# Attention probabilities transposed as products with the identity on two column strips, in one core's decoder kernel

## The chip, the core and the metric

The kernel runs on one core of a Trainium2 chip. The metric is the device time of one execution in microseconds, the median of several runs. TensorE (PE in the profile, with its weight loads as PEld) does the products and transposes, VectorE (DVE) and ScalarE (ACT) the elementwise work, GpSimd (POOL) and SyncE (SP) mostly issue transfers.

## The reference

Two decoder layers over 512 tokens of width 1024. Each is half a SwiGLU block, a mixing block with sparse attention (8 heads of 64), a pooling branch and attention into 256 memory tokens (4 heads of 64), and another half SwiGLU block. What the change touches is the last product of both attentions:

```python
logits = jnp.einsum('bqhd,bqkhd->bhqk', qb, kg).astype(jnp.float32) * (HEAD_DIM ** -0.5)
logits = jnp.where(valid[:, None], logits, -jnp.inf)
p = jax.nn.softmax(logits, axis=-1).astype(vg.dtype)
return jnp.einsum('bhqk,bqkhd->bqhd', p, vg)
...
p = jax.nn.softmax(logits, axis=-1).astype(mv.dtype)
out = jnp.einsum('bhsm,bmhd->bshd', p, mv)
```

## The kernel before

Activations lie transposed: features on the partitions, tokens along the columns. The large products (the SwiGLU blocks and the projections) split both operands into a high and a low part of type fp32r and add three products; their weights stream from memory through a ring of four slots. They take up most of the time.

The attention of a layer is cut into 48 units. A unit `n` is one head of one tile of 128 queries; the tiles go from the last to the first, and each has 8 sparse heads and then 4 memory heads. A sparse head of query tile `i` has `i + 1` blocks of 128 keys, a memory head has two. So a layer has 8 x (4 + 3 + 2 + 1) + 16 x 2 = 112 blocks, and the two layers 224.

Each unit passes four stages:

- `logits(n)` on TensorE, two units side by side: the product over 64 rows, for the two heads of a pair in the two halves of the rows (`64*128` in the profile's shapes: 64 rows by 128 columns of the array).
- `mask_and_max(n)` on VectorE (L1364) adds the mask and takes the maximum; `exps(n)` on ScalarE (L1086) takes the exponential and writes `prob[n % 4]` (in t1 or in buffers of their own, so the profile names it `t` or `prob`).
- `transpose_p(n)` on TensorE (L821): each block of probabilities, queries by keys, is transposed to keys by queries into `bank[2 + n % 2]`. `copy_pt` then copies the bank to `pt[n % 4]`, for even units on ScalarE (L1079), for odd ones on VectorE (L344).
- `times_v(n)` on TensorE: for each block and each head of the pair the values (128 keys by 64) stand in the array, the transposed probabilities are streamed, and the two heads' results go to partitions 0 to 63 and 64 to 127 (`128*64`).

After a group of heads, `spread_sums(g)` spreads the inverse row sums in the same layout: a product of a broadcast column of `rinv` (128 by 64) with the identity, even units to the lower half of `bank[7]` and odd units to the upper half. There are 8 groups in a layer. ScalarE copies the result to `rt` (L1095), VectorE multiplies it in (L1382), and both split the result (L1102, L1392).

TensorE's order is written out by hand. One step of the loop takes two units, and so the stages of different units follow each other:

```python
for n in range(0, UNITS + LAG + 2, 2):
    ...
    if n < UNITS:
        logits(n)
    if n - 2 in group_after:
        spread_sums(group_after[n - 2])
    if 0 <= n - LAG < UNITS:
        transpose_p(n - LAG)
        transpose_p(n - LAG + 1)
    if 0 <= n - LAG - 2 < UNITS:
        times_v(n - LAG - 2)
```

`LAG` is 4 and `UNITS` 48. Transposes are followed directly by `times_v` in the steps n = 6 to 50, 23 times in a layer, and they directly follow `spread_sums` 8 times in a layer (n = 10, 14, 22, 26, 34, 38, 46, 50). Two pooling products (`pool_map`, with `wpool`) stand ahead of the logits of the steps 28 and 32; they share `bank[7]` and `bank[6]` with the sums and values, so they wait for the copy to `rt`. While the softmax runs, ScalarE also rounds weights for the output projection (`round_ahead`, L931 and L932, after the units 9, 11, 21 and 23).

`mm(out, lhsT, rhs)` is the plain product on TensorE (L472 is its line for all callers). All operands of the transposes, of `spread_sums` and of `times_v` are of type fp32.

Of the kernel before, what the change touches and what calls it, by code (L numbers as in the profile page):

```python
# [21 lines left out]
P = 128  # L22
# [3 lines left out]
HD = 64  # L26
# [43 lines left out]
C_ID = 0  # L70
# [35 lines left out]
def build(nc, x_t, mem_t, weights, pool_w, params, consts, out):  # L106
# [85 lines left out]
    prob = [t1[:, 0:T], t1[:, T:2 * T]] + \  # L192
# [7 lines left out]
    bank = [nc.alloc_psum_tensor(f"bank{i}", [P, 512], f32) for i in range(8)]  # L200
# [5 lines left out]
    def con(at, n=1, parts=P):  # L206
        return const[0:parts, at:at + n]
# [96 lines left out]
    def unit(n):  # L304
        s, h = divmod(n, UNITS_PER_TILE)
        i = TT - 1 - s
        is_mem = h >= HEADS
        return i, (h - HEADS if is_mem else h), is_mem, (MT if is_mem else i + 1)
# [44 lines left out]
    with nc.Block() as block:  # L353
# [111 lines left out]
        def _(pe):  # L465
# [5 lines left out]
            def mm(out_, lhsT, rhs, start=True, stop=True):  # L471
                return nc.tensor.matmul(out_, lhsT, rhs, start=start, stop=stop, skip_group_check=True)  # L472
# [126 lines left out]
            def mix(l):  # L599
# [73 lines left out]
                for i in range(TT):  # L673
                    last = mm(bank[3][:, TT + 4 * i:TT + 4 * i + 4], iw[0:4, i * P:(i + 1) * P],
                              con(C_ID, 4, 4))
# [9 lines left out]
                for i in range(MT):  # L685
                    last = mm(bank[2][:, i:i + 1], sq[:, i * P:(i + 1) * P], con(C_ONES, 1))
# [44 lines left out]
                for part, hr in enumerate((hr_hi, hr_lo)):  # L731
                    for s in range(QT):
                        rows = slice(s * STRIP, (s + 1) * STRIP)
                        last = mm(bank[4 + s][:, :], spread[rows, :], hr[rows, :], part == 0, part == 1)
# [7 lines left out]
                for c in range(MQT):  # L742
                    for i in range(MT):
                        last = nc.tensor.transpose(bank[4][:, c * MEM + i * P:c * MEM + (i + 1) * P],  # L744
                                                   mk_n[:, i * MEM + c * P:i * MEM + (c + 1) * P],
                                                   con(C_ID, P))
# [68 lines left out]
                def transpose_p(n):  # L815
                    i, h, is_mem, blocks = unit(n)
                    pe.wait_ge(p_ready, l * UNITS + (n + 1))
                    if n >= 2:
                        pe.wait_ge(pt_ready[n % 2], l * (UNITS // 2) + n // 2)
                    for b in range(blocks):  # L820
                        last = nc.tensor.transpose(bank[2 + n % 2][:, b * P:(b + 1) * P],  # L821
                                                   prob[n % 4][:, b * P:(b + 1) * P], con(C_ID, P))
                    last.then_inc(ptp_done, 1)

                def times_v(n):
# [37 lines left out]
                for n in range(0, UNITS + LAG + 2, 2):  # L863
                    if n in POOL_UNITS:
                        pool_map(POOL_UNITS.index(n))
# [9 lines that stand above are left out]
                    for b in FILL.get(n, ()):  # L875
                        fill(b)
# [641 lines left out]
```

## Time and profile before

| | us |
|---|---|
| median of 3 runs | 1970.55 (1969.13 to 1972.46) |
| the profiled execution, its own time | 1967.57 |
| its span | 1965.5 |
| TensorE busy | 1918.9 (98%) |
| ScalarE busy | 1082.7 (55%) |
| VectorE busy | 614.1 (31%) |

The span goes from the first instruction to the last; the rest of the execution's own time, 2.1 us, lies around it. Busy time of TensorE is read from modelled ends: one product's time runs into the next one's, so in a dense stretch the distance between the starts of two runs of products says what one costs, and not the time of one. The attention units of the first layer lie from 528 to 584 us of the span, those of the second from 1500 to 1556 us.

### The profile page before, as it was taken

The page shows a single profiled execution, that of the slowest core. Times are in us where ns is not written, and L with a number is a line of the kernel's source. Part 1 is how long each engine was busy: PE and PEld are TensorE (multiplying, and loading weights), DVE is VectorE, ACT ScalarE, POOL GpSimd, SP SyncE. Part 2 cuts the span into 40 slices and gives each one's busy share as a digit, 9 for nine tenths or more (in the row PEclk, how much of TensorE's full clock was granted, in tenths as well). Part 3 has the DMA queues.
Part 4 walks back from the last instruction along what each step waited for, and adds up shares of the span by engine and source line. Part 5 has one row for each costly group of instructions (what it writes and reads, how often), then busy time and mean ns, then how long its engine had stood idle before and what let it go on. Part 6 is the DMA issues. An engine that isn't in the chain of part 4 may idle for free.

```text
span 1965.5 us, 27449 instructions
## 1 busy us (share of the span) xinstructions
PE 1918.9 (98%) x9148; PEld 1559.4 (79%) x9148; DVE 614.1 (31%) x1176; ACT 1082.7 (55%) x1391; POOL 347.6 (18%) x400
## 2 busy tenths in 40 slices
PE   6999999999899999999999999999998999999999
PEld 4888888887668888888878888888876688888887
DVE  3222210367662322220052222004677542222101
ACT  6655543565475755553375556336656566565432
POOL 1111111112511111111111111111125011111110
PEclk9999999999999999999999999999999999999999
DMA  8988888788236888888868888888781279888887
GB/s 219 215 190 191 194 193 193 184 197 193 76 87 150 199 197 191 192 193 192 194 162 201 191 193 189 199 192 199 177 205 48 70 173 221 192 193 193 194 190 184
DMA packets 97703, 354.07 MB, mean 180 GB/s; under 512 B 10976, under 2 KB 11232, under 8 KB 97376
## 3 DMA queue, kind: packets, MB, share of 16 engines
q0 software_dynamic: 47232, 171.99, 49.2%
q1 hardware_dynamic: 49824, 178.81, 27.7%
q10 hardware_dynamic: 576, 2.36, 0.3%
q8 instruction: 40, 0.66, 0.1%
q14 instruction: 31, 0.25, 0.0%
HBM read 179.05 MB, written 2.10 MB: 92 GB/s over the span
## 4 chain that ended last, share of the span: by engine, by line
PE 94%; DMA 2%; DVE 1%; issue 1%; ACT 1%; DVEq 0%; SPq 0%; ACTq 0%; POOLq 0%
PE bank L472 92%; PE bank L821 1%; DMA w_lo<-raw 1%; DMA raw<-weights 1%; ACT w_lo L932 0%; DMA x<-x_t 0%; DVE z L1315 0%; DVE mk_n L1321 0%; ACT prob L1086 0%; DVE t L1364 0%; ACT kv L1049 0%; ACT t L1086 0%; ACT w_hi L931 0%; DVE pt L344 0%; PE bank L744 0%
## 5 line engine op out<-in xcount | busy, mean ns | idle before, releaser
L931 ACT ACTIVATE w_hi<-raw 128x1024 fp32r<-128x1024 f32 x329 | 348.4, 1059 | 617.6 <-PE bank L472 592.1
L472 PE MATMUL bank<-h_hi,w_hi 128*128 128x512 f32 x1664 | 656.0, 394 | 15.6 <-ACT h_hi L903 13.6
L472 PE MATMUL bank<-h_hi,w_lo 128*128 128x512 f32 x1664 | 651.5, 392 | 5.7 <-DMA w_lo<-raw 5.7
L472 PE MATMUL bank<-h_lo,w_hi 128*128 128x512 f32 x1664 | 634.3, 390 | 0.0
L395 POOL DMA_DIRECT2D w_lo<-raw x328 | 282.6, 863 | 1556.5 <-ACT w_lo L932 1517.3
L472 PEld LDWEIGHTS bank<-h_hi,w_hi 128*128 128x128 f32 x1664 | 314.9, 189 | 88.5 <-ACT h_hi L903 15.1
L472 PEld LDWEIGHTS bank<-h_hi,w_lo 128*128 128x128 f32 x1664 | 314.7, 189 | 71.9 <-DMA w_lo<-raw 6.2
L472 PEld LDWEIGHTS bank<-h_lo,w_hi 128*128 128x128 f32 x1664 | 313.2, 188 | 66.2 <-issue 1.4
L932 ACT ACTIVATE w_lo<-raw 128x1024 fp32r<-128x1024 f32 x329 | 342.8, 1042 | 0.0
L472 PE MATMUL bank<-a_hi,w_hi 128*128 (+1 forms) x832 | 324.6, 390 | 0.0
L472 PE MATMUL bank<-a_lo,w_hi 128*128 (+1 forms) x832 | 323.8, 389 | 0.0
L472 PE MATMUL bank<-a_hi,w_lo 128*128 (+1 forms) x832 | 323.7, 389 | 0.0
L1168 DVE SCALAR_TENSOR_TENSOR x<-bank,x 128x512 f32<-128x512 f32 x48 | 32.7, 691 | 512.9 <-PE bank L472 512.9
L472 PEld LDWEIGHTS bank<-a_hi,w_hi 128*128 128x128 f32 x832 | 156.2, 188 | 33.7 <-issue 1.4
L472 PEld LDWEIGHTS bank<-a_hi,w_lo 128*128 128x128 f32 x832 | 156.2, 188 | 32.5
L472 PEld LDWEIGHTS bank<-a_lo,w_hi 128*128 128x128 f32 x832 | 156.2, 188 | 32.0
L1186 DVE TENSOR_TENSOR t<-bank,r 128x512 f32<-128x512 f32 x88 | 60.8, 690 | 382.1 <-PE bank L472 382.1
L931 ACT ACT_TABLE_LOAD x45 | 57.7, 1283 | 126.8 <-PE bank L472 119.1
L1183 DVE TENSOR_TENSOR t<-bank,r 128x512 f32<-128x512 f32 x88 | 60.8, 691 | 161.2 <-PE bank L472 160.3
L1192 DVE TENSOR_TENSOR a_lo<-t,a_hi 128x512 f32 x88 | 60.9, 692 | 111.2 <-ACT a_hi L950 111.2
L1190 DVE TENSOR_TENSOR t<-t,t 128x512 f32<-128x512 f32 x88 | 60.9, 692 | 11.6 <-ACT t L947 1.6
L947 ACT ACT_TABLE_LOAD x44 | 56.5, 1283 | 0.8
(143 smaller groups left out, 1226.2 us busy)
## 6 DMA issues: line engine op xcount, KB each, us to landing
raw<-weights SPq DMA_DIRECT2D x332, 512.0 KB, 4.7
w_lo<-raw POOLq DMA_DIRECT2D x328, 512.0 KB, 5.8
x<-x_t SPq DMA_DIRECT2D x4, 512.0 KB, 7.1
mem<-mem_t ACTq DMA_DIRECT2D x2, 1024.0 KB, 7.4
out_t<-x SPq DMA_DIRECT2D x8, 256.0 KB, 2.2
const<-consts SPq DMA_DIRECT2D x1, 481.5 KB, 10.0
wpool<-pool_w ACTq DMA_DIRECT2D x2, 128.0 KB, 7.2
par<-params SPq DMA_DIRECT2D x1, 38.0 KB, 1.8
```

The source lines that it names most:

```text
L395: G.dma_start(w_lo[:, s], raw[:, s], accum_op=ALU.add).then_inc(w_ready[pos], 16)
L472: return nc.tensor.matmul(out_, lhsT, rhs, start=start, stop=stop, skip_group_check=True)
L821: last = nc.tensor.transpose(bank[2 + n % 2][:, b * P:(b + 1) * P], prob[n % 4][:, b * P:(b + 1) * P], con(C_ID, P))
L931: nc.scalar.activation(w_hi[:, s], raw[:, s], ACT.Copy).then_inc(w_hi_done, 1)
L932: nc.scalar.activation(w_lo[:, s], raw[:, s], ACT.Copy, scale=-1.0)\
L947: nc.scalar.activation(g, g, ACT.Silu).then_inc(silu_ready, 1)
L1168: V.scalar_tensor_tensor(out=chunk(x, j), in0=bank[j][:, :], scalar=scale, in1=chunk(x, j), op0=ALU.mult, op1=ALU.add)\
L1183: V.tensor_tensor(out=g, in0=bank[2 * half][:, :], in1=r[:, :], op=ALU.mult).then_inc(gate_ready, 1)
L1186: V.tensor_tensor(out=h, in0=bank[2 * half + 1][:, :], in1=r[:, :], op=ALU.mult).then_inc(gu_free, 1)
L1190: V.tensor_tensor(out=h, in0=g, in1=h, op=ALU.mult).then_inc(prod_ready, 1)
L1192: V.tensor_tensor(out=a_lo[:, ds(f * T + half * T, T)], in0=h, in1=a_hi[:, ds(f * T + half * T, T)].bitcast(f32), op=ALU.subtract).then_in ...
```

## The change

A block is no longer transposed with `nc.tensor.transpose` over the whole array, but with two plain products with the identity: the probabilities of 64 keys (128 queries by 64 keys) stand in the array, the identity (128 by 128) is streamed, and the result, 64 keys by 128 queries, goes to partitions 0 to 63 for the first half of the keys and 64 to 127 for the second.

```diff
                     for b in range(blocks):
-                        last = nc.tensor.transpose(bank[2 + n % 2][:, b * P:(b + 1) * P],
-                                                   prob[n % 4][:, b * P:(b + 1) * P], con(C_ID, P))
+                        for half in range(2):
+                            keys = b * P + half * HD
+                            last = mm(bank[2 + n % 2][half * HD:(half + 1) * HD, b * P:(b + 1) * P],
+                                      prob[n % 4][:, keys:keys + HD], con(C_ID, P))
                     last.then_inc(ptp_done, 1)
```

On TensorE, in the fourth of the steps with transposes (n = 10, query tile 3), the instructions stand as follows before (-) and after (+). `prob_95` and `prob_96` are the probabilities of the two units, `rinv` the inverse row sums, `pt_91` and `v` the operands of `times_v`; the numbers behind the names are the shape of the result.

```order
 L472 MATMUL bank<-const,rinv 64x128 x8
 L819 REGISTER_ALU
-L821 MATMUL bank<-const,prob_95 128x128 x4
-L817 REGISTER_ALU
-L821 MATMUL bank<-const,prob_96 128x128 x4
+L472 MATMUL bank<-const,prob_95 64x128 x8
+L817 REGISTER_ALU
+L472 MATMUL bank<-const,prob_96 64x128 x8
 L472 MATMUL bank<-pt_91,v 64x128
 L472 MATMUL bank<-pt_92,v 64x128
```

Nothing has moved; the eight transposes of two units have become 16 products of the shape of those on either side of them.

The same on TensorE in the step after the first group's sums of memory heads, where a unit has two blocks (n = 14).

```order
 L472 MATMUL bank<-const,rinv 64x128 x4
 L819 REGISTER_ALU
-L821 MATMUL bank<-const,prob_95 128x128 x2
-L817 REGISTER_ALU
-L821 MATMUL bank<-const,prob_96 128x128 x2
+L472 MATMUL bank<-const,prob_95 64x128 x4
+L817 REGISTER_ALU
+L472 MATMUL bank<-const,prob_96 64x128 x4
 L472 MATMUL bank<-pt_91,kv 64x128
```

Four transposes have become eight products. No other engine's instructions change.

## Rows read from the trace of the kernel before

**Rows 1.** The page: busy time by engine, and the chain that ended last

```profile
PE 1918.9 (98%) x9148; PEld 1559.4 (79%) x9148; DVE 614.1 (31%) x1176; ACT 1082.7 (55%) x1391; POOL 347.6 (18%) x400
...
PE 94%; DMA 2%; DVE 1%; issue 1%; ACT 1%; DVEq 0%; SPq 0%; ACTq 0%; POOLq 0%
```

**Rows 2.** Busy time in stretches (granted clock behind POOL): units of either layer

```profile
528.00:584.00 56.00, 53.03 (x542) 37.95 (x542) 39.10 (x136) 47.21 (x138) 18.80 (x23) 1.00 0.33 77
...
1500.00:1556.00 56.00, 52.62 (x538) 37.73 (x539) 39.47 (x137) 47.41 (x137) 19.36 (x23) 1.00 0.32 77
```

**Rows 3.** TensorE's groups by shape, whole span (x counts records)

```profile
L472 PE MATMUL bank<-pt,v 128*64 128x128 f32 x320 | 24.5, 283 | 0.0
L821 PE MATMUL bank<-const,t 128*128 128x128 f32 x112 | 18.9, 286 | 2.7 <-DVE pt L344 2.6
L821 PE MATMUL bank<-const,prob 128*128 128x128 f32 x112 | 17.6, 285 | 0.3
L472 PE MATMUL bank<-const,rinv 128*64 128x128 f32 x192 | 14.0, 281 | 0.0
...
L472 PE MATMUL bank<-pt,kv 128*64 128x128 f32 x128 | 10.5, 285 | 0.0
```

**Rows 4.** TensorE in order of time: start, us, line, shape, records (query tile 3)

```profile
533.49 1.09 PE L821 MATMUL bank<-const,t 128*128 128x128 f32 x8
534.51 1.09 PE L472 MATMUL bank<-pt,v 128*64 128x128 f32 x16
535.54 0.38 PE L472 MATMUL bank<-a_hi 64*128 64x256 f32 x2
...
536.09 1.09 PE L472 MATMUL bank<-const,rinv 128*64 128x128 f32 x16
537.11 1.09 PE L821 MATMUL bank<-const,prob 128*128 128x128 f32 x8
```

**Rows 5.** TensorE in order of time, query tile 2

```profile
553.11 0.88 PE L821 MATMUL bank<-const,prob 128*128 128x128 f32 x6
553.92 0.88 PE L472 MATMUL bank<-pt,v 128*64 128x128 f32 x12
554.72 0.50 PE L472 MATMUL bank<-a_hi 64*128 64x256 f32 x4
...
555.27 0.66 PE L821 MATMUL bank<-const,t 128*128 128x128 f32 x4
555.86 0.88 PE L472 MATMUL bank<-pt,v 128*64 128x128 f32 x12
...
558.01 0.66 PE L821 MATMUL bank<-const,prob 128*128 128x128 f32 x4
...
560.62 1.10 PE L472 MATMUL bank<-u,wpool 128*128 128x512 f32 x2 [1.38 <-ACT rt L1095]
```

**Rows 6.** TensorE's waits from 528 to 584 us: total, times, longest

```profile
PE bank L472 <- ACT rt L1095: 1.4, 1, 1.4
PE bank L821 <- DVE pt L344: 1.3, 3, 0.8
```

**Rows 7.** ScalarE in order of time: idle before (in brackets), around TensorE's longest wait

```profile
550.59 0.49 ACT L1079 ACTIVATE pt<-bank 128x384 f32<-128x384 f32 x1 [0.32 <-PE bank L821]
562.75 0.38 ACT L1079 ACTIVATE pt<-bank 128x256 f32<-128x256 f32 x1 [1.54 <-PE bank L821]
```

**Rows 8.** TensorE and VectorE around the second wait

```profile
543.85 1.13 DVE L1392 TENSOR_TENSOR a_lo<-yt,a_hi 128x512 fp32r<-128x512 f32 x1 [0.25 <-ACT a_hi L1102]
...
546.00 0.52 PE L821 MATMUL bank<-const,t 128*128 128x128 f32 x3 [0.76 <-DVE pt L344]
```

**Rows 9.** TensorE's three other waits inside a run of transposes, query tiles 1 and 0

```profile
566.71 0.92 PE L821 MATMUL bank<-const,t 128*128 128x128 f32 x4
...
575.89 0.30 PE L821 MATMUL bank<-const,t 128*128 128x128 f32 x1 [0.29 <-DVE pt L344]
...
579.02 0.30 PE L821 MATMUL bank<-const,t 128*128 128x128 f32 x1 [0.23 <-DVE pt L344]
```

## The prediction

> **What bounds the kernel now.** I read the page's first part and the chain first [rows 1]. TensorE is busy for 98% of the span and holds 94% of the chain that ended last, so a nanosecond of its work counts nearly in full wherever it does not stand ahead of a wait. The change touches only the attention units, so the second view is the one by stretches [rows 2]. In the 56 us of units of the first layer TensorE is busy for 53.03, in the same stretch of the second for 52.62; ScalarE comes next with 47. TensorE sets the pace here too, but it idles for 56.00 - 53.03 = 2.97 and 56.00 - 52.62 = 3.38 us, 6.4 together. The granted clock is 1.00 in both stretches, the 2.4 GHz level, with transposes in them as they are, so there is no clock for the change to win back here.
>
> The busy time of a group does not give the price of an operation, since the modelled times overlap. Therefore the third view is TensorE in order of time, and in it the distance from the start of one run to the start of the next. In the step at 533 us [rows 4] eight records of transposes start at 533.49 and the products with the values at 534.51: 1.02 us. Those are 16 records, and the next logits start at 535.54: 1.03 us. The 16 records of `spread_sums` at 536.09 hold the engine until 537.11: 1.02 us. In query tile 2 [rows 5] six transposes hold it from 553.11 to 553.92 (0.81), four from 555.27 to 555.86 (0.59); 12 records with the values from 553.92 to 554.72 (0.80).
>
> Two things follow from these lengths. From four transposes to eight is 0.59 to 1.02 us, so one costs (1.02 - 0.59) / 4 = 0.1075; from six to eight it is (1.02 - 0.81) / 2 = 0.105, from four to six (0.81 - 0.59) / 2 = 0.11. The starts are printed to 0.01 us; I take **0.109 us**. Twelve records of the other form to 16 is 0.80 to 1.02 or 1.03, 0.055 to 0.058 for one record, so two records cost what one transpose costs. And each run has a constant on top of its own work: 1.02 - 8 x 0.109 = **0.15 us**, for every one of these runs. It comes with each run whose form differs from the one before; all neighbours in these rows differ in form.
>
> **The number of records.** How many records a plain fp32 product leaves can be counted. The kernel has 224 blocks and as many transposes, and the trace 112 + 112 records of them: one each [rows 3]. There are 2 x 48 = 96 products in `spread_sums` and 192 records; 224 products with the values (one for each block of each unit) and 320 + 128 = 448 records. So a plain product of these fp32 operands takes two records, and costs 2 x 0.0545 = 0.109 us in a stretch in which the two halves of the columns alternate: 8 products of `spread_sums` in 1.02 us. A half-width product costs as much as a full-width transpose.
>
> **What the change removes.** 224 transposes at 0.109 us: -24.4 us.
>
> **What it adds.** 448 products at 0.109 us: +48.8 us. The nearest row is as near as can be: `spread_sums` also streams the identity (`const`, 128 columns, fp32), has 64 columns in the array over 128 rows, and its results go to the lower and upper half of a bank in turn. It differs only in that its stationary operand is a broadcast column. The products with the values have a real matrix there and show the same length [rows 4], so I take 0.109. The bounds: a pair of strips could share more than these rows do, and cost no more than the one transpose that it replaces (0.109 for two products); upward, 0.115, the dearer reading of two records above, which adds 448 x 0.006 = 2.7 us.
>
> **What it takes away between runs.** The transposes now have the same form, `128*64`, as what stands on either side of them. The run of transposes and the products with the values that follow become one run, and one of two constants goes: 23 times in a layer, 46 in all, 0.15 each, 6.9 us. Likewise `spread_sums` and the transposes behind it, 8 times in a layer, 16 x 0.15 = 2.4 us. Together -9.3 us. Bounds: nothing, if the constant belongs to something else (to the wait on a semaphore ahead of a run), and -9.3. Against the wait speaks that these runs show no idle time ahead of them [rows 4, 5]: what they wait for was there. The step from logits into the transposes stays a change of form, at the same price as logits into `spread_sums`.
>
> The sum on TensorE is 48.8 - 24.4 - 9.3 = **+15.1 us**. Copies, exponentials and waits are as many as before; what is queued behind `transpose_p` (the products with the values, then the next logits) comes later by the same time, and ScalarE and VectorE get each bank later by up to the length of one unit's added work: 4 x 0.109 = 0.44 us in query tile 3, where a step is 2.6 us long (from 533.49 to 537.11, less the 1.02 us of `spread_sums` [rows 4]). They have a whole step until their copies are read.
>
> **What is absorbed.** Added work ahead of a wait costs nothing, as long as what releases the wait was not itself behind the added work. The waits of a layer are the 1.4 us of the pooling product for `rt`, and three waits of transposes for VectorE's copy, 1.3 us together [rows 6].
>
> - The pooling product, 1.38 us, at 560.62 [rows 5]. `rt` is copied by ScalarE, and ScalarE last waits for TensorE at 550.59 and then not until 562.75 [rows 7]: it is busy throughout, with exponentials, copies and the weights' rounding. So what TensorE adds in between is hidden: the second unit of the run that the copy at 550.59 belongs to (three blocks less a constant, 0.18), the runs at 553.11 (six blocks less two constants, 0.35), at 555.27 (four less one, 0.29) and 558.01 (four less two, 0.14), 0.96 us if ScalarE never comes to wait, half of that if it does. I take 0.8.
> - The transposes at 546.00 wait 0.76 us for a copy behind VectorE's split of the first group's result [rows 8], which goes back by ScalarE and VectorE to the last products of that group with the values, two steps earlier. Behind these stand one run of four blocks less two constants and the first two blocks of the run itself, 0.14 + 0.22 = 0.36.
> - The other two, 0.29 and 0.23, and a short one inside the run at 566.71 (0.92 where four transposes show 0.66 elsewhere) [rows 5, 9], take the blocks of the unit ahead of them: 0.22 + 0.11 + 0.11 = 0.44.
>
> That is 1.6 us in a layer, 3.2 in both. The bounds are nothing, and all of TensorE's idle time, 6.4, or 7.4 with the share of each wait that the modelled ends cover. 1.6 is what these paths allow; I keep both ends.
>
> **The result:** +15.1 - 3.2 = **+11.9 us**. Against the profiled execution's own 1967.57 us that makes 1979.5. The runs' median is 3.0 above that execution, and the same sum on it is 1982.4; I predict **1982**.
>
> **The rivals.**
>
> - **Faster: a pair of half-width products for the price of one transpose.** The mechanism is on TensorE alone: the two strips take the identity at the same time, and as a product with ones and zeros it might leave one record instead of two. Then the added term falls to the removed one, and only the constants are left: 1967.57 - 9.3 = 1958.3, or 1961 on the median. It decides as soon as a pair takes less than 0.109 + 9.3 / 224 = 0.15 us. Against it stands `spread_sums`, which streams this identity in this layout and takes 0.218 for a pair. 6 in 100.
> - **No change: the attention is held by ScalarE and VectorE after all.** ScalarE is busy for 47 of 56 us [rows 2], and without a pause from 550.59 to 562. If all idle time is taken up and the constants are worth somewhat more than read (0.2 instead of 0.15), it is 48.8 - 24.4 - 12.4 - 7.4 = +4.6, near the bound of what can be told, 3.9. 3 in 100.
> - **Much slower: the plain product is far dearer than the transpose.** Then a block costs 0.436 us instead of 0.109, if each product takes four times a transpose and the strips lie side by side: 224 x 0.327 = 73.2, less 9.3, +64 us, 2034 on the median. For it speaks nothing in the rows: `spread_sums` takes a half of that. 2 in 100. The Trainium skill gives this ratio (the page "TensorE: Matmul & The Clock Gate", section Terms): transpose mode is "4× faster for FP32". By that rule the sum would be +64 us; the trace has two records for one and 0.218 for 0.109, a factor of two.
> - **Slower than forecast: the constants stay.** If they are the price of a run's first wait, not of the change of form, only 24.4 - 3.2 = +21.2 is left, 1992. For it: each run in these rows has both, a new form and a wait in the program. 6 in 100.
> - **Slower than forecast: the chain of both engines.** A unit's transposes end up to 0.44 us later, ScalarE starts its copy later, and its exponentials stand behind that copy. If in query tiles 1 and 0 (12 steps in a layer) the engines then wait for each other in turn, nothing is absorbed and some 0.1 to 0.2 us is added in each of 24 steps: +15.1 + 3.6 = +18.7, 1989. Against it: probabilities are made two steps before they are read. 8 in 100.
>
> **How the numbers follow.** The forecast has 75 in 100. Its range goes from all waits absorbed (+7.7) to none (+15.1), on the median 1978.3 to 1985.7. With 1.5 us to either side for the spread of the runs (the median of before came from 1969.13 to 1972.46), and 2.7 above for the dearer reading, the range is **1976.5 to 1990**; the case of the chain lies in it. What a measurement of this kernel can tell from no change is about 0.2%, 3.9 us. Slower by more: the forecast, the dear product, the constants that stay and the chain of engines, 0.75 + 0.02 + 0.06 + 0.08 = 0.91; the same: 0.03; faster: 0.06.
>
> **What would show it.** In the profile after, the transposes' group should have 896 records of shape `128*64`, `const,t` and `const,prob`, at L472. In the step of rows 4 the run of transposes should take 16 x 0.109 = 1.74 us and the products with the values behind it 0.87 + 0.15, with starts that follow the transposes without an extra gap; the run behind `spread_sums` likewise. The span from 528 to the last unit should be longer by some 6 us in each layer, and TensorE's wait for `rt` shorter by 0.5 to 1 us. The stretches outside the attention should be as long as before. I am wrong if a pair of strips takes other than 0.218 us, if the gap ahead of the values stays, or if ScalarE's idle time grows while TensorE's doesn't shrink.

## The result and the profile after

The changed kernel takes 1980.33 us (median of 7 runs, 1977.35 to 1986.45), the one before 1969.51 (7 runs, 1964.89 to 1973.76). The ratio is 1.0057, with a 95% interval of 1.0039 to 1.0075: slower by 10.8 us (7.7 to 14.8 by the interval). The profiled execution took 1982.62 us, its span is 1980.7.

First the page of the changed kernel, which answers to [rows 1].

```profile
PE 1937.3 (98%) x9820; PEld 1587.2 (80%) x9820; DVE 615.1 (31%) x1176; ACT 1083.2 (55%) x1391; POOL 347.6 (18%) x400
...
PE 94%; DMA 2%; issue 1%; DVE 1%; ACT 1%; DVEq 0%; SPq 0%; ACTq 0%; POOLq 0%
```

TensorE has 672 records more, 896 in place of 224, and 18 us more of busy time; the others are within 1 us of what they were. Then the groups by shape, as in [rows 3].

```profile
L472 PE MATMUL bank<-const,t 128*64 128x128 f32 x448 | 30.5, 279 | 0.0
L472 PE MATMUL bank<-const,prob 128*64 128x128 f32 x448 | 28.9, 274 | 0.0
...
L472 PE MATMUL bank<-pt,v 128*64 128x128 f32 x320 | 23.0, 273 | 0.0
L472 PE MATMUL bank<-const,rinv 128*64 128x128 f32 x192 | 14.0, 281 | 0.0
```

The step of [rows 4], TensorE in order of time, with the changed kernel's own times:

```profile
535.25 1.97 PE L472 MATMUL bank<-const,t 128*64 128x128 f32 x32
537.04 1.04 PE L472 MATMUL bank<-pt,v 128*64 128x128 f32 x16
538.02 0.38 PE L472 MATMUL bank<-a_hi 64*128 64x256 f32 x2
...
538.56 1.09 PE L472 MATMUL bank<-const,rinv 128*64 128x128 f32 x16
539.49 1.92 PE L472 MATMUL bank<-const,prob 128*64 128x128 f32 x32
541.23 1.04 PE L472 MATMUL bank<-pt,v 128*64 128x128 f32 x16
542.21 0.62 PE L472 MATMUL bank<-a_hi 64*128 64x384 f32 x4
```

From the first transpose to the next logits it is 538.02 - 535.25 = 2.77 us; before, it was 535.54 - 533.49 = 2.05. The added 0.72 us are eight blocks at 0.109 less one constant of 0.15. With `spread_sums` in the step, the whole takes 542.21 - 538.56 = 3.65, which is 8 + 16 + 8 slots of 0.109 us and one constant of 0.15 (3.64), where the kernel before paid three.

To measure a layer I use the stretch from its first transpose to its last product with the values ("the unit stretch" below). The view by stretches (length; busy time of TensorE, weight loads, VectorE, ScalarE, GpSimd; granted clock) for the kernel before:

```profile
528.77:589.71 60.94, 57.97 (x581) 41.51 (x580) 40.59 (x137) 48.11 (x139) 18.11 (x22) 1.00 0.30 71
1501.32:1562.25 60.93, 57.98 (x581) 41.52 (x580) 40.59 (x137) 48.10 (x139) 18.12 (x22) 1.00 0.30 71
```

and for the changed one:

```profile
529.12:595.27 66.15, 65.17 (x918) 54.14 (x916) 41.00 (x137) 48.34 (x139) 18.12 (x22) 1.00 0.28 66
1511.32:1577.46 66.14, 65.16 (x917) 54.12 (x916) 40.99 (x137) 48.34 (x139) 18.11 (x22) 1.00 0.28 66
```

The unit stretch has grown by 5.2 us in each layer, 10.4 in both: nearly the whole difference of the medians, 10.8. TensorE's busy time in it is up by 7.2 us, its idle time down from 2.97 to 0.98. The waits that are left, as in [rows 6] (the changed kernel's lines below L821 are numbered two higher):

```profile
PE bank L472 <- ACT rt L1097: 0.9, 1, 0.9
```

The three waits for VectorE's copy are gone from this list, and the one for `rt` has gone from 1.4 to 0.9 us.

The profiled execution's span is 15.2 us longer than before's, not 10.4. Nearly all of the rest is in the projections of the second layer, ahead of its units: 1396.3 to 1491.1 us, where the kernel before needed from 1390.9 to 1480.4. Both, the changed one first:

```profile
1396.30:1491.10 94.80, 88.64 (x404) 69.09 (x405) 66.49 (x162) 48.73 (x69) 22.60 (x23) 0.96 0.75 178
```

```profile
1390.90:1480.40 89.50, 85.22 (x405) 66.84 (x405) 66.46 (x162) 48.71 (x69) 22.59 (x23) 0.99 0.80 189
```

The granted clock there was 0.96 on average instead of 0.99. Whether that belongs to the change is asked below.

### The profile page after: what moved, and what is told of

It is laid out like the page before. It is cut to its first block, busy times and chain, and to the rows that moved or that the text cites. A ratio compares the mean times of both kernels' runs of the same rounds, so it can differ in the third digit from the quotient of the medians.

```text
span 1980.7 us, 28793 instructions
## 1 busy us (share of the span) xinstructions
PE 1937.3 (98%) x9820; PEld 1587.2 (80%) x9820; DVE 615.1 (31%) x1176; ACT 1083.2 (55%) x1391; POOL 347.6 (18%) x400
## 4 chain that ended last, share of the span: by engine, by line
PE 94%; DMA 2%; issue 1%; DVE 1%; ACT 1%; DVEq 0%; SPq 0%; ACTq 0%; POOLq 0%
PE bank L472 94%; DMA w_lo<-raw 1%; DMA raw<-weights 1%; DMA x<-x_t 0%; ACT w_lo L934 0%; DVE z L1317 0%; ACT t L1088 0%; DVE mk_n L1323 0%; ACT kv L1051 0%; ACT w_hi L933 0%; PE bank L744 0%; DVE top L1258 0%; ACT prob L1088 0%; DVE score L1261 0%; DVE mk_sq L1307 0%
```

## The experiments

**The array whole, but plain products (full_plain).** One product of 128 by 128 in place of the two strips:

```diff
-                        for half in range(2):
-                            keys = b * P + half * HD
-                            last = mm(bank[2 + n % 2][half * HD:(half + 1) * HD, b * P:(b + 1) * P],
-                                      prob[n % 4][:, keys:keys + HD], con(C_ID, P))
+                        last = mm(bank[2 + n % 2][:, b * P:(b + 1) * P],
+                                  prob[n % 4][:, b * P:(b + 1) * P], con(C_ID, P))
```

> Each block is transposed by one plain fp32 product with the identity over the whole array (128 by 128), not on two column strips. It has as many records as the changed kernel (two for each block, where the strips have four in two lanes), but its form is not that of the runs beside it. My account (0.109 us for each of the two records of a block, 0.15 us for each change of form): the 0.109 is paid as in the changed kernel, the 62 constants stay. From the first transpose to the last product with the values 66.1 + 31 x 0.15 = 70.8 us in each layer, where the kernel before has 60.9 and the changed one 66.1; in all about 20 us above the kernel before, ratio 1.010. Rival, the constant is the price of the first wait of a run and the strips saved nothing but that they hide it by chance: the stretch is as in the changed kernel, 66.1, and the ratio 1.0055. Rival, a plain product over the whole array costs as much as the transpose and only the strips are dear: 60.9 us, ratio 1.000.

Measured: 1989.31 us (4 runs) against 1970.08 (17 runs), ratio 1.0099, interval 1.0085 to 1.0114. The unit stretches, and the step of [rows 4] in this kernel:

```profile
528.85:601.90 73.05, 72.63 (x694) 58.07 (x692) 41.14 (x136) 48.04 (x137) 17.25 (x21) 0.98 0.25 59
1512.09:1583.42 71.33, 70.91 (x693) 56.45 (x692) 41.15 (x137) 48.47 (x139) 18.06 (x22) 1.00 0.26 61
```

```profile
537.00 2.05 PE L472 MATMUL bank<-const,t 128*128 128x128 f32 x16
538.98 1.09 PE L472 MATMUL bank<-pt,v 128*64 128x128 f32 x16
540.01 0.39 PE L472 MATMUL bank<-a_hi 64*128 64x256 f32 x2
```

In the second layer, at the full clock, it is 71.3 us, against 70.8 expected; the first layer has a lower mean clock (0.98) and 1.7 us more. So a plain product is what costs, with strips or without: two records for a block; their single starts (the start of each record in the trace, which the view gathers into one line) lie 0.112 us apart in this step. (They are 448 in all; the changed kernel has 896 in two lanes, so "as many records" in the expectation was wrong.) The strips give back 71.3 - 66.1 = 5.2 us in a layer. By the forecast's price 31 x 0.15 = 4.7 of them are the constants; the 224 records of 0.112 instead of 0.109 us are worth another 0.7. The step shows it as well: transposes and values together take 540.01 - 537.00 = 3.01 us here and 2.77 in the changed kernel. Of these 0.24 us one constant is 0.15 and the dearer records are 0.05. Both rivals fall.

**The same strips, one after the other (strips_in_turn).** The two loops exchanged:

```diff
-                    for b in range(blocks):
-                        for half in range(2):
+                    for half in range(2):
+                        for b in range(blocks):
```

> The changed kernel with the loops exchanged: all blocks of a unit for the lower half of the partitions first, then all for the upper. The same products, records and forms. My account: a pair costs 0.218 us because the two strips stream side by side, each record 0.109 us in its own strip. Products that follow each other in the same strip then take 0.218 each, and the transposes of a layer 112 x 0.436 = 48.8 us instead of 24.4: the stretch from the first transpose to the last product with the values grows from 66.1 to about 88 us (86 to 91, since at each change of strip one record still runs beside another), the whole kernel by 40 to 49 us over the changed one. Rival, a record costs 0.0545 us wherever it goes, since only 64 columns are written: 66 us, the time of the changed kernel.

Measured, one execution each: 1989.02 us, and 1993.45 in the second. The unit stretches of the first:

```profile
528.47:598.47 70.00, 69.12 (x917) 58.21 (x916) 41.19 (x137) 48.31 (x139) 18.06 (x22) 1.00 0.27 62
1512.40:1583.87 71.47, 70.59 (x917) 59.68 (x916) 41.16 (x136) 48.25 (x139) 17.93 (x22) 0.98 0.26 61
```

That is 3.9 us more than the changed kernel where the clock was full, and neither account had it: mine said about 22, the rival none. Why it is so little stands in the order of starts, a step of query tile 3:

```profile
535.78 2.24 PE L472 MATMUL bank<-const,t 128*64 128x128 f32 x29
537.75 0.32 PE L472 MATMUL bank<-pt,v 128*64 128x128 f32 x1
537.86 0.27 PE L472 MATMUL bank<-const,t 128*64 128x128 f32 x1
537.91 0.27 PE L472 MATMUL bank<-pt,v 128*64 128x128 f32 x1
537.97 0.27 PE L472 MATMUL bank<-const,t 128*64 128x128 f32 x1
538.02 0.27 PE L472 MATMUL bank<-pt,v 128*64 128x128 f32 x1
538.08 0.27 PE L472 MATMUL bank<-const,t 128*64 128x128 f32 x1
538.13 1.09 PE L472 MATMUL bank<-pt,v 128*64 128x128 f32 x13
539.15 0.39 PE L472 MATMUL bank<-a_hi 64*128 64x256 f32 x2
```

Products with the values, which stand behind all transposes in the program, start before the last transposes: they go to the lower strip, which is free, while the last transposes still wait for the upper one. So the strips do run side by side, and a later product for the free strip overtakes earlier ones for the busy strip. The view does not name the strips; I tell them apart by their pace. The last transposes start at 537.86, 537.97 and 538.08, the products with the values between them at 537.91, 538.02 and 538.13: two lanes, each with 0.11 us from record to record. The step takes 539.15 - 535.78 = 3.37 us, 0.60 over the changed kernel's 2.77. In the single starts the second lane's first record comes at 536.27, 0.49 us after the first lane's, and from there its 24 records follow almost without a pause, so this late start is most of the 0.60. My account was right in that each strip has its own pace of 0.109 us for a record, and wrong in that strips run only beside their direct neighbour.

> strips_in_turn once more. Its two layers took 70.0 and 71.5 us from the first transpose to the last product with the values, against 66.1 in both for the changed kernel, and the second had a window of the lower clock inside. If that window is the difference, the layers without one take 70.0 again; the price of taking the strips in turn is then 3.9 us in a layer. Rival, the order of the strips gives different lengths without it.

The second execution has the same two layers, 70.00 us at a clock of 1.00 and 71.69 at 0.97; the 3.9 us stand.

**One record instead of two (full_fp32r).** As full_plain, with `prob` and an identity `ident` of type fp32r:

```diff
-                                  prob[n % 4][:, b * P:(b + 1) * P], con(C_ID, P))
+                                  prob[n % 4][:, b * P:(b + 1) * P], ident[:, :])
```

> As full_plain, but the probabilities are written as fp32r (rounded, so the result is less exact) and multiplied with an fp32r identity, whole array, one record for each block. If the number of records sets the price, it is 0.109 us for a block as for a transpose, and the stretch is as before, 60.9 us, ratio 1.000. Rival, the type sets the price: products of 512 columns in fp32r start about 0.23 us apart, that is some 0.057 for 128 columns; then a block costs half, up to 6 us go from each layer, less what turns into waits for ScalarE and VectorE: 56 to 58 us, ratio 0.996. Rival, the weight load of fp32r is longer (188 ns in the trace, 140 for the transposes' fp32): up to 0.15 us for a block and some 3 us more in each layer.

Measured: 1979.76 us (4 runs), ratio 1.0059, interval 1.0035 to 1.0082. The four runs go from 1976.22 to 1988.75 us. The transposes' group (line numbers are two higher in this kernel) and the unit stretches:

```profile
L474 PE MATMUL bank<-ident,prob 128*128 128x128 f32 x224 | 39.9, 306 | 2.4 <-DVE pt L346 2.1
```

```profile
530.46:591.38 60.92, 58.08 (x582) 44.19 (x580) 40.59 (x137) 48.17 (x139) 18.11 (x22) 1.00 0.30 71
1503.43:1574.55 71.12, 68.73 (x582) 52.05 (x580) 40.49 (x136) 47.71 (x137) 17.37 (x21) 0.83 0.26 61
```

The first layer settles what was asked: with one record a block, the stretch is that of the transposes, 60.92 against 60.94. It is the second record that costs, and neither the type's stream nor its load. The second layer is 10.2 us longer, at a granted clock of 0.83 (parts of it at the lower level, 1.2 GHz), which none of the accounts foresaw; so the time of this kernel as a whole says nothing about the transposes' price.

> full_fp32r once more. In its first profile the units of the first layer took 60.92 us, as with the transposes, and those of the second 71.11, with TensorE's granted clock at the lower level for stretches inside them. If the lower clock comes from what stood ahead of the units in that execution (as in every kernel here, whose clock falls for a window or two before the units), it can be elsewhere or absent this time: 60.9 us in the layers without it. Rival, the fp32r products themselves bring it about: it is low inside the units of the second layer again, with some 5 to 10 us more there.

Again 60.93 us in the first layer at 1.00, and 71.10 in the second at 0.83. It repeats, so it is not an accident of one execution. The other kernels' unit stretches show 0.97 to 1.00, those with the transposes 1.00. Where the clock is low in the second layer, the first execution's own times (the unit stretch begins at 1503.43):

```profile
1500.30:1503.43 3.13, 2.07 (x10) 0.84 (x6) 1.78 (x8) 2.41 (x8) 2.97 (x4) 0.54 0.03 5
1503.43:1517.40 13.97, 13.97 (x86) 11.76 (x86) 6.67 (x19) 7.47 (x17) 12.99 (x17) 0.50 0.00 1
...
1541.30:1551.50 10.20, 10.20 (x46) 5.99 (x45) 4.03 (x14) 4.19 (x14) 0.00 (x0) 0.51 0.50 130
```

The clock falls 3 us ahead of the layer's first fp32r transpose, in a stretch where TensorE idles for a third of the time, and stays low for 17 us; it falls once more inside the units. The second execution has the same pattern, 3 us ahead as well. So the first fall is not the doing of this layer's fp32r transposes. But it lasts far longer than the low stretches just ahead of the units in the other kernels (3.4 or 6.8 us), and the second fall, 38 us into the units, has no counterpart in any of them. Neither of the two accounts is shown, and why the second layer and not the first stays open.

**The sums behind the transposes (sums_behind).** In the kernel before, a cheaper way to drop a constant:

```diff
-                    if n - 2 in group_after:
-                        spread_sums(group_after[n - 2])
                     if 0 <= n - LAG < UNITS:
                         transpose_p(n - LAG)
                         transpose_p(n - LAG + 1)
+                    if n - 2 in group_after:
+                        spread_sums(group_after[n - 2])
```

> The kernel before, with its transposes as they were; only the sums of a group (spread_sums) are issued behind the transposes of their step instead of ahead of them, so that they stand directly before the products with the values, which have the same form. My account: one constant of 0.15 us goes, 8 times in a layer: 60.9 becomes 59.7 us in each layer, -2.4 us in all, ratio 0.9988. Rival, the copy of the sums to rt comes later on ScalarE (the run of transposes is 0.4 to 0.9 us long), ScalarE and with it the pooling product wait for it: 0 to +1 us in each layer. Rival, the constant belongs to the first wait of a run: no change in the dense steps.

Measured: 1969.51 us (12 runs), ratio 0.9994, interval 0.9984 to 1.0004: no difference that can be told. The profile tells more: TensorE in the step with sums, then its waits in the units of the first layer.

```profile
537.17 1.09 PE L821 MATMUL bank<-const,prob 128*128 128x128 f32 x8
538.20 1.09 PE L472 MATMUL bank<-const,rinv 128*64 128x128 f32 x16
539.12 1.04 PE L472 MATMUL bank<-pt,v 128*64 128x128 f32 x16
540.09 0.44 PE L472 MATMUL bank<-a_hi 64*128 64x384 f32 x2
```

```profile
PE bank L821 <- DVE pt L344: 1.7, 3, 1.0
PE bank L472 <- ACT rt L1095: 0.9, 1, 0.9
PE bank L821 <- ACT pt L1079: 0.9, 1, 0.9
```

The constant goes as expected: sums and values together take 540.09 - 538.20 = 1.89 us where two runs of this length took 2.05. But the unit stretches, 60.55 and 60.52 us, are only 0.4 shorter instead of 1.2. The transposes' waits for copies have grown to 1.7 and 0.9, from 1.3 and none that was listed, while the one for `rt` has shrunk from 1.4 to 0.9: 0.8 us more in all. That is the part of the 1.2 that did not arrive; the saving turned into waits. The rival that the constant belongs to a run's first wait falls, since the dense step has become shorter.

**Without the pooling on GpSimd (before_no_pooling, after_no_pooling).** To see why the wait at 546 us [rows 8] vanished altogether; the body of `pooling` is left out of both kernels.

> The kernel before without the pooling on GpSimd (left out: the running sums, their scaling and the subtraction; the pooled values are the unpooled ones). In the kernel before, VectorE's split of the first group's result took 1.13 us beside a GpSimd tensor operation and 0.69 in the changed kernel, where GpSimd was done by then, and TensorE's wait of 0.76 us at 546 us (0.93 by the starts) went altogether, where I had it shortened by 0.36. My account now: that wait is GpSimd's doing and falls to at most 0.3 us here; from the first transpose to the last product with the values 60.0 to 60.5 us in the first layer, against 60.9. Rival, the wait comes from ScalarE, which waits for VectorE and is held by the weights' rounding: it stays, 60.9.

> The changed kernel without the pooling on GpSimd (left out as in the run beside it). The changed kernel has no wait left there, so it should hardly gain: 66.0 to 66.1 us as with the pooling. The difference between the two kernels without pooling is then 5.6 to 6.1 us in a layer instead of 5.2, near the 5.95 that was predicted. Rival: both gain alike and the difference stays at 5.2.

Measured, one execution each: 1970.43 and 1983.20 us. TensorE's waits in the units and VectorE's split of the first group, kernel before without pooling (line numbers are 16 lower in it):

```profile
PE bank L456 <- ACT rt L1079: 1.4, 1, 1.4
PE bank L805 <- DVE pt L344: 0.8, 3, 0.3
```

```profile
543.68 0.69 DVE L1376 TENSOR_TENSOR a_lo<-yt,a_hi 128x512 fp32r<-128x512 f32 x1 [0.25 <-ACT a_hi L1086]
```

The split takes 0.69 us instead of 1.13, the longest wait for VectorE falls from 0.76 to 0.3, and the unit stretches are 60.52 and 60.48. The changed kernel stays at 66.11 and 66.10. Without pooling the change costs 5.6 us in a layer. So 0.4 of the 0.76 us were GpSimd's doing. In the changed kernel GpSimd's tensor operation ends at 544.78 us and the split starts at 546.62, 2.8 us later than in the kernel before: GpSimd is already done.

**The changed kernel once more (after_again).**

> The changed kernel once more, for the stretch of the projections of the second layer (from the first index products to the transposes of the memory keys): 94.7 us in its first profile against 89.5 before, in the first layer 91.6 against 90.8. My account: this is not the change's, but scatter of the projections' weights and waits from run to run; here it comes out near 89 to 92. Rival: the later start of the second layer does it, and it is 94.7 again.

Measured: 1979.57 us (4 runs), ratio 1.0057, interval 1.0036 to 1.0077. The unit stretches are 66.11 and 66.12. The projections of the first and of the second layer:

```profile
417.00:510.30 93.30, 88.35 (x404) 69.14 (x404) 66.46 (x162) 48.73 (x69) 22.55 (x23) 0.96 0.76 181
1396.40:1487.30 90.90, 85.07 (x404) 66.89 (x404) 66.44 (x162) 48.73 (x69) 22.55 (x23) 1.00 0.79 186
```

This time the first layer has the clock of 0.96 and 93.3 us, and the second 1.00 and 90.9. Most of the extra time in the projections goes with the clock and changes its place between executions: TensorE is busy there for 88.6 and 88.4 us at 0.96, and for 85.1 to 85.2 at 0.99 to 1.00, with the change or without. Its idle time in these stretches, 4.3 to 6.2 us, varies as well and follows neither the layer nor the change. So the 94.8 us are not tied to the later start of the second layer, and the 10.4 us of the units account for nearly all of the 10.8 between the medians. I take the rest for scatter; an interval of 7.7 to 14.8 us does not exclude a few us of it.

## Why the prediction was right

The forecast was +11.9 us, to 1982; measured were +10.8, 1980.3, in the range.

- **The price of a pair of strips**, 0.218 us for a block instead of 0.109: right. Eight blocks between neighbours of their own form take 541.23 - 539.49 = 1.74 us, full_plain paid it without strips, and full_fp32r, with one record, did not. The dear product (+64) and the pair for one transpose (-9.3) have fallen. The 0.0545 us for one record in the forecast is no price of its own: strips_in_turn shows two lanes side by side with 0.109 us for a record in each.
- **The constants**, 0.15 us for 46 + 16 changes of form: right. The step shows one where there were two, full_plain has them back (5.2 us in a layer, of which 4.7 by the constants), and sums_behind shows one go with the transposes untouched. That they are the price of the first wait has fallen.
- **The sum on TensorE**, +7.55 us in a layer: its busy time rose by 7.2. Busy time is no exact test of it, since the modelled ends cover a part of each wait (at 546 us 0.76 are listed of 0.95 by the starts), and that part went with the waits. By the starts each run of products changed as the sum has it: eight blocks behind logits and ahead of the values +0.77 and the values' run -0.05, which is 0.72 together.
- **What is absorbed** was mis-sized: I had 1.6 us in a layer. The idle time fell by 1.99, and the growth of 5.2 us instead of 7.55 makes it some 2.3 by the starts; so 5.2 us are left instead of 5.95. The largest miss is the wait at 546 us. I gave it the work that now stands between its cause and itself, 0.36 us; but it had a second cause, a GpSimd operation beside VectorE's split, at a time that TensorE does not set. It went altogether, 0.76 us as listed. The small waits later in the layer gave up some 0.8 us by the starts instead of 0.44, with one of 0.2 us at 557 us among them that no list shows. The wait for `rt` erred the other way, 0.5 us gone instead of 0.8, since ScalarE came to wait for TensorE in between, which the forecast had named as the lower case. ScalarE in the changed kernel, idle time in brackets, to the copy to `rt` that the pooling product waits for:

```profile
551.79 0.49 ACT L1081 ACTIVATE pt<-bank 128x384 f32<-128x384 f32 x1 [0.48 <-PE bank L472]
...
554.45 0.49 ACT L1081 ACTIVATE pt<-bank 128x384 f32<-128x384 f32 x1 [0.91 <-PE bank L472]
...
557.99 0.49 ACT L1081 ACTIVATE pt<-bank 128x384 f32<-128x384 f32 x1 [0.18 <-PE bank L472]
...
564.26 0.38 ACT L1097 ACTIVATE rt<-bank 128x256 f32<-128x256 f32 x1
```

- **The other two rivals.** The chain of both engines has not come up: no new wait of TensorE is listed, and by the starts the new ones are about 0.1 us each, late in the layer. "All idle time is taken up" has not either: 0.98 us of it is left in each layer, and the constants are 0.15 us, not 0.2.
- **One line of what to look for was off:** I gave the values' run the whole constant (0.87 + 0.15); it is 0.98 us, and 0.05 of the constant lies in the transposes' run (1.79 instead of 1.74, which the run behind `spread_sums` takes). So a constant is paid in two parts, 0.05 inside the run that begins and 0.10 on leaving.

## What to carry to other kernels

Before replacing an operation by one with a better layout, count its records against those of a neighbour of the target's form: here the plain fp32 product had two for the transpose's one, and 224 x 0.109 us of work outweighed 62 x 0.15 us of saved changes. A saved gap on the pacing engine is worth its full length only where no wait for another engine follows: of 1.2 us that sums_behind took off a layer, 0.4 arrived.

## What the runs showed that I had not expected

- On column strips TensorE does not keep the program's order between strips: products with the values started up to 0.3 us ahead of transposes that stand before them (537.75 against 538.08). Strips taken in turn cost 3.9 us in a layer, not the 22 of my account, in which strips run only beside their direct neighbour.
- Plain fp32r products of the whole array (128 columns) in place of the transposes came with a granted clock of 0.83 in the units of the second layer, twice, and 10.2 us there; the first layer had 1.00. No other kernel fell below 0.97 in its unit stretches. The clock fell 3 us ahead of that layer's first such product, so that layer's transposes did not start it; why it stayed low and fell again is open.
- VectorE's split of 128 by 512 at 543.85 us took 1.13 us beside a GpSimd tensor operation (until 544.43), and 0.69 with GpSimd's pooling taken out.
